# Differential attention of one transformer layer: row maxima taken bank by bank, scores packed in five PSUM banks, a head's later steps spread over three turns

## What is computed

```python
def diff_softmax_attend(q, k, v, lam):
    s = jnp.einsum("bhmqd,bhmkd->bhmqk", q, k, preferred_element_type=jnp.float32) * (A_HEAD_DIM ** -0.5)
    p = jax.nn.softmax(s, axis=-1)
    a = p[:, :, 0] - lam * p[:, :, 1]
    return jnp.einsum("bhqk,bhkd->bhqd", a.astype(v.dtype), v)
...
    def finish(o):
        return (rms_norm(o, subln_w, SUBLN_EPS) * (1.0 - lambda_init)).reshape(o.shape[0], o.shape[1], A_WIDTH)
```

## Time and profile before

| | us |
|---|---|
| median of three runs | 2889.46 |
| the profiled execution, its own time | 2896.26 |
| its span in the profile | 2894.5 |
| the attention block in it | some 285, from 964 to 1250 |
| TensorE busy, of the span | 2591.4 |
| VectorE busy | 1242.6 |
| ScalarE busy | 578.2 |

### The profile page before, as it was taken

How to read it: one execution, slowest core, us unless ns; L and a number is a source line. 1 busy time by engine, 2 the same in 40 slices (tenths; PEclk the granted TensorE clock), 3 DMA queues, 4 the chain that set the end, 5 groups by cost and what they waited for, 6 DMA issues and landing times. The chain is left out here.

```text
span 2894.5 us, 57389 instructions
## 1 busy us (share of the span) xinstructions
PE 2591.4 (90%) x23169; PEld 1344.1 (46%) x23169; DVE 1242.6 (43%) x2089; ACT 578.2 (20%) x1089; POOL 477.6 (16%) x719
## 2 busy tenths in 40 slices
PE   4999858888898778889999999999599999999996
PEld 2444457776444455544444444445334443443442
DVE  2466655654763466611885211116522222222221
ACT  4333222222220466610000110012100000000000
POOL 0011145552110000000000000000023332332332
PEclk8999968999999999999999999999699999999998
DMA  6011010000010000030222222112487999959532
GB/s 233 22 34 32 1 47 11 19 18 31 22 43 0 15 0 0 0 80 1 84 77 77 69 77 91 45 36 102 180 317 254 351 374 386 361 208 366 200 84 76
DMA packets 198499, 320.02 MB, mean 111 GB/s; under 512 B 13600, under 2 KB 135943, under 8 KB 198119
## 3 DMA queue, kind: packets, MB, share of 16 engines
q1 hardware_dynamic: 183175, 294.11, 28.0%
q0 software_dynamic: 15168, 23.60, 3.7%
HBM read 299.63 MB, written 22.50 MB: 111 GB/s over the span
## 5 line engine op out<-in xcount | busy, mean ns | idle before, releaser
L2651 PE MATMUL p_gate_up<-w_unit,rowsT 128*32 128x512 f32 x4672 | 520.1, 596 | 17.6 <-DVEq L2693 8.1
L1988 PE MATMUL p_gate<-hT,w_gate 128*128 128x512 f32 x768 | 342.1, 598 | 7.0 <-DVE region L2112 5.9
L2651 PEld LDWEIGHTS p_gate_up<-w_unit,rowsT 128*32 128x32 f32 x4672 | 155.0, 111 | 338.6 <-issue 311.1
L2665 PE MATMUL p_y<-w_unit,hiddenT 128*32 128x256 f32 x4672 | 267.4, 381 | 1.2 <-DVE hiddenT L2707 1.2
L1034 PE MATMUL p_w<-hT,w_c 128*128 128x512 f32 (+1 forms) x640 | 248.7, 550 | 0.0
L1988 PEld LDWEIGHTS p_gate<-hT,w_gate 128*128 128x128 f32 x768 | 144.0, 191 | 183.1 <-issue 181.4
L2537 DVE STREAM_TRANSPOSE rows_turned<-rows 128x256 f32<-128x256 f32 x74 | 33.0, 445 | 450.3 <-PE p_gate_up L2651 445.6
L2665 PEld LDWEIGHTS p_y<-w_unit,hiddenT 128*32 128x32 f32 x4672 | 155.6, 110 | 130.3 <-issue 44.5
L1034 PEld LDWEIGHTS p_w<-hT,w_c 128*128 128x128 f32 x640 | 121.5, 190 | 124.9 <-issue 121.6
L2688 ACT ACTIVATE sigmoid<-p_gate_up 128x256 f32<-128x256 f32 x73 | 28.1, 385 | 744.6 <-PE p_gate_up L2651 744.6
L2137 DVE SCALAR_TENSOR_TENSOR region<-gated,taps,region x120 | 154.1, 1284 | 16.7 <-DVE region L2134 1.3
(11 more groups left out here) (368 smaller groups left out, 3510.3 us busy)
## 6 DMA issues: line engine op xcount, KB each, us to landing
w_unit<-in_w_gate SPq DMA_DIRECT2D x128, 512.0 KB, 14.7
w_unit<-in_w_up SPq DMA_DIRECT2D x128, 512.0 KB, 16.3
w_unit<-in_w_down SPq DMA_DIRECT2D x128, 512.0 KB, 11.4
w_b<-in_w_mod SPq DMA_DIRECT2D x32, 512.0 KB, 4.6
w_gate<-in_w_in SPq DMA_DIRECT2D x24, 512.0 KB, 4.0
region<-in_w_mod SPq DMA_DIRECT2D x4, 2048.0 KB, 15.2
w_c<-in_w_in SPq DMA_DIRECT2D x16, 512.0 KB, 3.9
w_branch<-in_w_branch SPq DMA_DIRECT2D x24, 256.0 KB, 4.4
```

The lines of the kernel that those rows point to most:

```text
L1988: last = nc.tensor.matmul(p_g[half][:, :], wg[i][:, c, :], k.hT[:, c, CTX + at:CTX + at + 512], start=(c == 0), stop=(c == KD - 1))
L2651: last = nc.tensor.matmul(p_gu[part, :].rearrange("p (m c r) -> p m c r", m=2, r=BLK), xT[:, c, :], unit[:, :, j], start=(c == 0), stop=(c ...
L2665: last = nc.tensor.matmul(p_y[part, 0:W], hT[:, c, :], k.ring[u % UNITS][:, c % 2, W * j:W * j + W], start=(c == 0), stop=(c == KD - 1))
```

## The change

Only `attend` is changed. In the words of the new code, with j from 0 to 31:

- All 32 turns are written out; there is no loop, no `q_block` and no GpSimd work. TensorE reads the queries from `qT` in place.
- The scores of both maps lie end to end in one tensor of five banks: map 0 in columns 0 to 1279, map 1 in 1280 to 2559. The third bank holds the last 256 columns of map 0 and the first 256 of map 1. `scores` issues in a new order and signals as parts land; the piece of map 0 that shares a bank waits for map 1's (`scored_low`).
- `maxima` takes four reductions and a small maximum in place of two reductions: 512 columns of map 0, the shared bank's 2 x 256, 512 of map 0, and 1024 of map 1.
- In turn j TensorE issues scores(j+1), the last transpose group of j-2, any output transposes, weigh(j-2), and the first two groups of j-1. Weigh has a PSUM bank of its own (`p_out`), `aT` is one buffer in place of two, and `p` of map 0 has three.
- ScalarE's turn is store groups 0 and 1 of j-2, save(j-3), store group 2 of j-2, any outputs, any root, exps(j+1). VectorE's is sums(j), maxima(j+1), mix(j), any norm.
- Roots are taken for query blocks 0 and 1, 2 and 3, 4 and 5 together, and for 6 and for 7 alone: 5 in place of 8.

```diff
+    BATCHES = [(0, 1), (2, 3), (4, 5), (6,), (7,)]
...
+        p_s = k.ps(st, "p_scores", [P, 2560])
...
+                def scores(j):
+                    after(pe, "exped", j - 1, 2, 1)
+                    q, h = divmod(j, HEADS)
+                    for m, at, size, name in ((1, 0, 256, "scored_low"), (0, 0, 512, "scored_first"), (1, 256, 512, None),
+                                              (0, 1024, 256, "scored_tails"), (0, 512, 512, "scored0"),
+                                              (1, 768, 512, "scored1")):
+                        rows = slice(64 * m, 64 * m + 64)
+                        if at == 1024:
+                            after(pe, "scored_low", j)
+                        mm = nc.tensor.matmul(score(m, at, size), k.qT[rows, h, q * P:q * P + P],
+                                              k.kT[rows, h, at:at + size], start=True, stop=True)
+                        if name:
+                            mm.then_inc(s(name), 1)
+
+                def turn(j, g):
+                    at, size = GROUPS[g]
+                    if g == 0:
+                        after(pe, "mixed", j)
+                        after(pe, "stored", j - 1, 3, 2)
+                    elif g == 1:
+                        after(pe, "stored", j - 1, 3, 1)
+                    else:
+                        after(pe, "stored", j, 3, 0)
+                    for t in range(size):
+                        last = nc.tensor.transpose(p_t[g % 2][:, t * P:(t + 1) * P],
+                                                   pm[0][j % 3][:, (at + t) * P:(at + t + 1) * P], k.c("ident"))
+                    last.then_inc(s("turned"), 1)
+
...
-                queries(None, True, False)
-                queries(Pass(s, pe, 0, per), True, False)
-                with pe.Fori(1, NQ - 1) as it:
-                    queries(Pass(s, pe, it, per), False, False)
-                queries(Pass(s, pe, NQ - 1, per), False, True)
-                turn_outputs(Pass(s, pe, NQ - 1, per))
+                scores(0)
+                for j in range(N + 2):
+                    if whole(j + 1):
+                        scores(j + 1)
+                    if whole(j - 2):
+                        turn(j - 2, 2)
+                    q = outputs_in(j)
+                    if q is not None:
+                        turn_outputs(q, j - 2)
+                    if whole(j - 2):
+                        weigh(j - 2)
+                    if whole(j - 1):
+                        turn(j - 1, 0)
+                        if q is not None:
+                            after(pe, "y_stored", q)
+                        turn(j - 1, 1)
...
+                exps(0)
+                for j in range(N + 3):
+                    if whole(j - 2):
+                        store(j - 2, 0)
+                        store(j - 2, 1)
+                    if whole(j - 3):
+                        save(j - 3)
+                    if whole(j - 2):
+                        store(j - 2, 2)
+                    if outputs_in(j) is not None:
+                        store_outputs(outputs_in(j))
+                    for i, qs in enumerate(BATCHES):
+                        if j - 3 == HEADS * qs[-1] + HEADS - 1:
+                            take_root(i)
+                    if whole(j + 1):
+                        exps(j + 1)
+                for q in range(NQ):
+                    if outputs_in_tail(q):
+                        store_outputs(q)
...
+                def maxima(j):
+                    def reduce(to, ap):
+                        ch.run(nc.vector.tensor_reduce(to, ap, AX.X, ALU.max))
+
+                    def bound(m):
+                        after(dve, "exped", j - 2, 2, m)
+                        n = 2 * (j % 2) + m
+                        nc.vector.tensor_scalar(nb[:, n:n + 1], part[:, 3:4], part[:, m:m + 1], -SCALE, ALU.max,
+                                                ALU.mult).then_inc(s("maxed"), 1)
+
+                    after(dve, "scored_first", j)
+                    reduce(part[:, 2:3], score(0, 0, 512))
+                    after(dve, "scored_tails", j)
+                    reduce(part[:, 0:2], p_s[:, 1024:1536].rearrange("p (m n) -> p m n", m=2))
+                    ch.run(nc.vector.tensor_tensor(part[:, 0:1], part[:, 0:1], part[:, 2:3], ALU.max))
+                    after(dve, "scored0", j)
+                    reduce(part[:, 3:4], score(0, 512, 512))
+                    bound(0)
+                    after(dve, "scored1", j)
+                    after(dve, "maxed", j, 2, 0)
+                    reduce(part[:, 3:4], score(1, 256, 1024))
+                    bound(1)
+                    after(dve, "maxed", j, 2, 1)
+
+                def sums(j):
+                    n, h = 2 * (j % 4), j % HEADS
+                    after(dve, "exped", j, 2, 1)
+                    after(dve, "saved", j - 4)
+                    ch.run(nc.vector.reciprocal(inv[:, n:n + 2], total[:, n:n + 2]))
+                    nc.vector.scalar_tensor_tensor(ratio[:, h:h + 1], inv[:, n + 1:n + 2], k.rows[:, 32:33],
+                                                   total[:, n:n + 1], ALU.mult, ALU.mult).then_inc(s("summed"), 1)
+
+                def mix(j):
+                    a, b, h = pm[0][j % 3], pm[1][j % 2], j % HEADS
+                    after(dve, "summed", j)
+                    nc.vector.scalar_tensor_tensor(a[:, :], b[:, :], ratio[:, h:h + 1], a[:, :], ALU.mult, ALU.add) \
+                        .then_inc(s("mixed"), 1)
+
+                def norm(i):
+                    low, size = batch_heads(i)
+                    after(dve, "rooted", i)
+                    if i:
+                        after(dve, "y_turned", BATCHES[i - 1][-1])
+                    ch.run(nc.vector.reciprocal(rinv[:, 0:size], root[:, 0:size]))
+                    nc.vector.tensor_tensor(o_n[:, 0:size, :], o_raw[:, low:low + size, :],
+                                            rinv[:, 0:size].unsqueeze(2).to_broadcast([P, size, P]), ALU.mult) \
+                        .then_inc(s("normed"), 1)
+
+                maxima(0)
+                for j in range(N + 4):
+                    if whole(j):
+                        sums(j)
+                    if whole(j + 1):
+                        maxima(j + 1)
+                    if whole(j):
+                        mix(j)
+                    for i, qs in enumerate(BATCHES):
+                        if j - 3 == HEADS * qs[-1] + HEADS - 1:
+                            norm(i)
 
 
```

250 lines of the change are left out of this document (88 added, 162 removed).

## The result

| us | before | after |
|---|---|---|
| median (4 runs each, same chip) | 2891.43 (2887.97 to 2895.81) | 2866.3 (2864.54 to 2874.5) |
| after / before | | 0.9913, 95% interval 0.9899 to 0.9927 |
| profiled execution, its own time | 2896.26 | 2864.54 |
| attention block, first operation to the end of its last | 284.65 | 255.32 |
| TensorE's idle time ahead of ordinary scores | 0.33 | 0.20 |

The kernel became faster by 25.1 us, 0.87%. The two profiles differ by 31.7, and the block alone by 29.3. First the windows of the kernel after: busy PE, PEld, DVE, ACT and POOL, then the granted clock, DMA and GB/s.

What follows compares the result with a forecast made beforehand. The order of waits bounds the block, with both full maxima behind all scores. 7.85 + 3 x 8.85 + 27 x 6.70 + 29.0 = 244.3 against 284.6; less 6 for clock, gain 34: 2855, range 2847 to 2871.

Steps and rivals of the forecast that it cites:

- every case of the clock: Attention block: TensorE's lower clock costs 0 to 16 us, 6 taken; own range 2847 to 2864, 66 in 100.
- two rivals, which did not come about: TensorE's chain takes over (2865 to 2872, 17 in 100); new VectorE pieces cost more (2864, 10 in 100).
- the sign of being right: In the profile after, the attention block would take 246 to 254 us.
- scaling to 3.74; 1024 columns 3.77: VectorE, ordinary head: first scaling ends 3.74 us after the scores' start, and the 1024-column reduction starts at 3.77.
- the new pieces cost more than their length: VectorE: each of three more operations costs 0.1 over forecast, 0.3 a head, 9 in all, 2864; 10 in 100.
- TensorE's chain: TensorE's work in an ordinary head: scores, transposes, third store with handovers and weigh, 6.65 us against an interval of 6.70.
- both rivals on TensorE: Halves fall out of step (2909, 5 in 100); chain takes over without loss of halves (2865 to 2872, 17 in 100).
- a piece could wait for its neighbour's start: TensorE score products: with matmuls in program order, a piece might wait for its neighbour's start, never for its end.
- Roots: ScalarE ahead of the exps: each root adds 2.15 us; three of five lengthen an interval to 8.85.
- Start and tail: Ends of the block: first interval 7.85 us; tail 29.0 from the last scores, 7.2 longer than before's 21.8.
- The clock: TensorE at its lower clock: 1.65 us for each of three slow scores, and 1 for the tail, 6 in all.
- The three slow scores of the forecast: scores(1), scores(2) and one of the three after a root, at the lower clock, 1.65 us each.

Runs made afterwards that it cites:

- e8_split_scaling: Changed kernel with each of the two scalings split into a maximum and a plain scaling: 7.10 us an interval, block 261.9, 2872.3 in one run.
- e5_halves_in_turn: Changed kernel with all map 1 score products issued ahead of map 0's, not by turns: 8.16 us an interval, block 297.9, 2904.2 in one run.
- e6_fill_start: Changed kernel plus 44, 32 and 20 unread transposes behind scores(0) and in the first two turns: block 252.0 us, 2864.3 in one run.
- e7_fill_roots: Changed kernel with the second transpose group issued five times in the three turns with a root: block 253.4 us, 2863.2 in one run.
- the repeat: Changed kernel run again without any change: median 2870.32 us, 0.9913 of before, block 255.2.
- both fills: Two runs of the changed kernel with extra transposes, at the start (block 252.0 us) and beside the roots (block 253.4 us).
- the three-block version: Changed kernel with roots for blocks 0-2, 3-5, 6 and 7, norm in place, extra transposes at start and roots: 2861.41 us, 0.9886 of before, block 247.7.
- e4_mix_first: Changed kernel with VectorE's mix of head j put back ahead of the maxima of head j+1: 7.62 us an interval, block 272.3, 2876.2 in one run.
- e2_eight_roots: Changed kernel with eight roots, one for each query block, in place of five: block 265.4 us, 2879.6 in one run.

## Why the prediction was right, and what was mis-sized

The forecast was 2855.0 with 2847 to 2871; measured 2866.3, inside, and faster as said. The mechanism held step by step; the median stands 11.3 above the forecast. It comes apart so: with a fourth run (2895.81) the median of the kernel before stands 2.0 higher (2891.43 against 2889.46), the block gained 29.3 and not 34.3, and 4.2 of the block's gain isn't in the medians (25.1).

That the time is inside is in part luck. The prediction gives its own mechanism, with every case of the clock, 2847 to 2864, and 2866.3 lies 2.3 above that. It is within the whole range because two rivals, which did not come about, had widened it. The block's 255.3 lies 1.3 above the 246 to 254 named as the sign of being right.

**The ordinary head: 6.84, not 6.70.** Times from the start of the scores, forecast against the timeline of the head at 1061.18:

| | forecast | measured |
|---|---|---|
| first reduction | 1.24 | 1.17 |
| small maximum | 2.68 | 2.62 |
| third reduction | 2.86 | 2.81 |
| first scaling | 3.59 | 3.54 |
| 1024 columns | 3.77 | 3.86 |
| second scaling | 5.03 | 5.12 |
| second exp | 5.23 | 5.37 |
| next scores | 6.70 | 6.84 |

The term that was mis-sized is "scaling to 3.74; 1024 columns 3.77", priced like the old L917 at 0.15, with the next operation 0.04 behind it. The new L946 takes two columns as operands and lasts 0.21, and the 1024 columns start 0.11 behind its end: 0.14 more, of which 0.06 is length and 0.07 the gap. The gap is 0.11 in `e8_split_scaling` too (1038.85, 0.15 long, to 1039.11), so it goes with that place, where the code has two waits, and not with the kind of scaling. Which of the waits it is, the trace's single records show. VectorE's wait for its own scaling (`maxed`; it keeps the reduction from overwriting the scaling's input) is an instruction by itself there: the signal comes at 3.76, the instruction runs at 3.79, the reduction starts 0.07 later. Ahead of the third reduction the like instruction waits for scores that have landed, and is through at 2.65, before the small maximum has ended. A second column for the maximum would make the wait needless; that was not tried. At the second scaling 0.05 more is the length alone. The earlier first reduction gives 0.07 back. Over 27 ordinary intervals it is 3.8. The rival "the new pieces cost more than their length" was right in kind, and 0.14 a head where it said 0.3: the two scalings do, the reductions do not (512 in 0.69, 1024 in 1.22, each starting 0.03 to 0.04 behind its forerunner, as forecast). The adding of an operation in `e8_split_scaling` shows that this chain has no slack.

**TensorE's chain** was put at 6.65. It is the interval less its wait, 6.84 - 0.20 = 6.64. It did not take over, and scores took 2.42 in the new order, so both rivals on TensorE fell. `e5_halves_in_turn` shows what the order of the pieces is worth. The prediction's reading that a piece could wait for its neighbour's start is not what happened there: map 0's half did not wait for map 1's later starts, only its signals came late.

**Roots:** 8.90 - 6.84 = 2.06, forecast 2.15; three ahead of ordinary scores and one ahead of the last exps, as forecast. The rule of the Trainium skill on the table load ("ScalarE: Activation LUTs", "What ACT_TABLE_LOAD costs", 1.38 more for a drain at each switch) is again not borne out: the load at 1041.82 took 1.28 and the root started at 1043.11, 0.01 after its end; the exp started 0.02 after the second load's.

**Start and tail:** first interval 7.91 against 7.85; tail 29.44 against 29.0 and 1 for the clock.

**The clock** was put at 5 outside the tail and took 6.4: 2.24 and 1.30 at the start (2.29 and 1.30 between scores), and 1.42 behind each of two roots. The three slow scores of the forecast were four. `e6_fill_start` and `e7_fill_roots` give these back, 3.3 and 2 x 1.40.

**Sum of the block:** forecast 250.3. To it, from the start of the block on: 3.8 for ordinary heads, 1.4 for the clock, 0.2 for the roots, 0.1 for the first interval, 0.2 for the one of 7.08, and 0.6 less in the tail: 255.4, measured 255.3. The one interval of 7.08 (the ninth) came back at the same place in four other profiles (the repeat, both fills, the three-block version), and 0.25 and 0.36 more stand there in `e5_halves_in_turn` and `e4_mix_first`. The other four variants have nothing there, and `e8_split_scaling` has such a one (7.45 among 7.10) later on. Its third reduction started 0.25 late, 0.27 behind the last signal that it waited for; the cause is open.

**The 4.2 outside the block** stay open. That code is the same in all kernels, but not its time: in the eleven profiles of the changed kernel and its variants the block began between 954.8 and 969.2, and what lies outside the block took 2602 to 2617 in one execution. A difference of 4 is within that. The interval of the ratio reaches from 21 to 29 us, and the block's 29.3 lies at its edge.

**Where the gain comes from.** Counted between the starts of scores, the block's 29.3 are made up so: 31 intervals shorter by 0.59 are 18.3. The seven intervals with a root were 29.1 above an ordinary one before; now three such and the two slow scores behind them are 9.1, which gives 20.0. The start loses 1.1 (slower scores, less the copy of the queries), the tail is 7.6 longer, and the 7.08 is 0.2. So the roots give as much as all the ordinary heads. `e2_eight_roots` puts 10.1 of it on there being fewer; the rest is that one costs 2.06 and not 4.02.

The 0.59 itself is a difference: the first reduction starts 1.37 earlier (1.17 after the scores, 2.54 in the earlier trace rows), but from there to the second exp four reductions and a small maximum take 4.20, where two full ones took 3.42. The loop has no part in it: in the first block of before, written out too, an ordinary interval was 7.43 as well.

Each of three parts, undone alone, lengthens the block: the overlap with the scores by 42.6, the mix behind the maxima by 17.0, the spreading by 17.1. These are no shares of 29.3, because each is taken out of a kernel that still pays for the others. Without the overlap, the 0.78 that the smaller pieces cost stays. And the mix cost nothing where it stood before, since it ended at 2.07 and the maxima could not start until 2.54; it is in the way only once they start at 1.17. It takes the parts together: the overlap brings VectorE's chain to within 0.20 of TensorE's, and the others clear VectorE and ScalarE ahead of it. The packing into five banks, the weigh's own bank and the queries read in place were not undone alone.

## What to carry to other kernels

Where a reduction waits for a whole row of products, cut it at bank borders and start it at the first; but count each added small operation by the start of the next one, taken from a row with the same operands, because on the deciding chain one of 0.15 to 0.21 in length costs 0.19 to 0.32 in every turn. Issue first the products whose signal is wanted first: in the other order the signal came 0.8 after its product had ended. Before an order is spread over turns, list what each engine has ahead of the step that decides, in the turn with the rare work (a root) too. And where rare work leaves TensorE idle, look at the scores behind it: at the lower clock they cost 1.3 to 2.3 each, and work that nobody reads gives that back.

## What was not expected of the hardware

- A TENSOR_SCALAR of 128x1 with two column operands takes 0.21 us, with a constant 0.15, and a TENSOR_TENSOR of two columns 0.16.
- Products of unequal width on the two row halves run side by side: 2.42 for six in the alternating order, 2.95 with all of one half issued first, where one behind the other would be 4.3 (an estimate of the prediction's).
- A product's signal waits for those issued ahead of it, though they are on the other row half: 2.47 for one that ended at 1.66, behind a 2.43.
- After 5.49 and 4.49 of TensorE's idle time the scores took 4.64 and 4.01 at the start. After 2.28 of idle at each of three roots they took 2.42 (1047.51, granted clock 1.00), 3.87 (1104.26) and 4.02 (1162.44); ahead of the slow ones the clock was still 1.00, and it fell to 0.50 only 0.8 and 0.7 after they had started (0.50 from 1105.2 to 1108.2). What decides between the two was not settled.
